# Three transformer blocks in one fp32 kernel on one Trainium2 core: the second block's down sections in the paired, token-major form

## The reference

```python
# second block
x = x + einsum('btc,cd->btd', merged, w_out)
h2 = rms_norm(x, norm2_g)
ff = square(relu(einsum('btd,df->btf', h2, w_ff1)))     # 2048 -> 8192
x = x + einsum('btf,fd->btd', ff, w_ff2)                # 8192 -> 2048
return rms_norm(x, final_g)
# third block: begins with rmsnorm(x, norm_mix_g), ends with
h = rmsnorm(x, norm_mlp_g)
x = x + square(relu(h @ w_up)) @ w_down
return rmsnorm(x, norm_final_g)
```

## Time and profile before

| what | value |
|---|---|
| median of three runs | 3273.06 us (3272.34 to 3274.05) |
| the profiled execution | 3272.41 us |
| its span | 3270.6 us, granted clock 0.999 |
| PE busy | 3248.7 us (99%), 21227 matmuls |
| PEld busy | 2816.8 us (86%) |
| DVE busy | 2264.7 us (69%), 3011 instructions |
| ACT busy | 1553.9 us (48%) |
| POOL busy | 359.0 us (11%) |
| DMA queue of the weights | 591.51 MB, 57.2% of 16 engines' span |

### The profile page before, as it was taken

The page is one execution under the profiler, slowest core; times in us unless marked ns, Lnnn a source line. Parts: engine busy times, 40 slices in busy tenths (PEclk is TensorE's granted clock), DMA queues, the critical chain, the costliest instruction groups (busy, mean ns, idle before and its releaser), DMA issues.

```text
span 3270.6 us, 51798 instructions
## 1 busy us (share of the span) xinstructions
PE 3248.7 (99%) x21227; PEld 2816.8 (86%) x21227; DVE 2264.7 (69%) x3011; ACT 1553.9 (48%) x2109; POOL 359.0 (11%) x356
## 2 busy tenths in 40 slices
PE   9999999999999999999999999999999999999999
PEld 8888888888878888888888888888888888888887
DVE  6468666567487667776665456656778777877787
ACT  5355434444554455445444444444455544544455
POOL 3000233310102003311000000012000100000000
PEclk9999999999999999999999999999999999999999
DMA  8455443446546557566656555665555555565555
GB/s 253 149 183 181 140 137 126 139 163 230 183 145 206 168 174 227 173 181 189 195 188 196 190 182 185 190 192 189 177 177 168 180 181 183 201 209 182 188 203 180
DMA packets 541729, 595.08 MB, mean 182 GB/s; under 512 B 25429, under 2 KB 484021, under 8 KB 540982
## 3 DMA queue, kind: packets, MB, share of 16 engines
q1 hardware_dynamic: 541350, 591.51, 57.2%
q10 hardware_dynamic: 144, 0.26, 0.0%
HBM read 585.32 MB, written 6.32 MB: 181 GB/s over the span
## 4 chain that ended last, share of the span: by engine, by line
PE 95%; DVE 3%; ACT 1%; issue 1%; POOL 0%; DMA 0%; SPq 0%; POOLq 0%; DVEq 0%; ACTq 0%
PE gp L3107 49%; PE gp L3111 26%; PE gp L2984 7%; PE gp L2990 4%; PE sidep L1340 3%; PE sidep L3009 1%; PE gp L3009 1%; PE sidep L3014 1%; DVE w_parts L2909 1%; PE gp L3014 1%; PE sidep L1626 0%; PE sidep L1630 0%; PE sidep L1908 0%; DMA high<-x 0%; PE sidep L2046 0%
## 5 line engine op out<-in xcount | busy, mean ns | idle before, releaser
L2909 DVE TENSOR_TENSOR w_parts<-ring,w_parts 128x1024 fp32r<-128x1024 f32 x1036 | 1305.3, 1285 | 250.3 <-ACT w_parts L2897 248.2
L3107 PE MATMUL gp<-x_parts,w_parts 128*128 128x512 f32 x5264 | 1296.6, 394 | 0.0
L2897 ACT ACTIVATE w_parts<-ring 128x1024 fp32r<-128x1024 f32 x1036 | 1058.0, 1052 | 302.3 <-PE gp L3107 125.1
L3107 PEld LDWEIGHTS gp<-x_parts,w_parts 128*128 128x128 f32 x5264 | 959.0, 188 | 186.0 <-issue 2.5
L3111 PEld LDWEIGHTS gp<-x_parts,w_parts 128*128 128x128 f32 x5264 | 684.7, 191 | 36.8 <-issue 4.9
L3111 PE MATMUL gp<-x_parts,w_parts 128*128 128x256 f32 x5264 | 708.4, 284 | 1.0 <-DVE w_parts L2909 0.4
L2317 ACT ACTIVATE lo_half<-gp 128x512 f32<-128x512 f32 x220 | 131.5, 598 | 721.2 <-PE gp L3107 586.5
L3107 PE MATMUL gp<-ff_parts,w_parts 128*128 128x512 f32 x1792 | 430.4, 391 | 0.0
L3107 PEld LDWEIGHTS gp<-ff_parts,w_parts 128*128 128x128 f32 x1792 | 328.9, 188 | 63.3
L2480 DVE TENSOR_TENSOR stage<-gp,lo_half 128x512 f32<-128x512 f32 x168 | 115.9, 690 | 291.4 <-ACT lo_half L2317 289.4
L3111 PEld LDWEIGHTS gp<-ff_parts,w_parts 128*128 128x128 f32 x1792 | 231.0, 191 | 10.4 <-issue 0.9
(11 more groups left out here) (435 smaller groups left out, 2640.7 us busy)
## 6 DMA issues: line engine op xcount, KB each, us to landing
ring<-w_in SPq DMA_DIRECT2D x440, 512.0 KB, 4.3
ring<-w_ff SPq DMA_DIRECT2D x256, 512.0 KB, 4.5
ring<-w_up SPq DMA_DIRECT2D x128, 512.0 KB, 4.2
ring<-w_down SPq DMA_DIRECT2D x128, 512.0 KB, 5.5
ring<-w_out SPq DMA_DIRECT2D x96, 512.0 KB, 4.4
ring<-w_branch_attn SPq DMA_DIRECT2D x16, 512.0 KB, 4.5
ring<-w_branch_rwkv SPq DMA_DIRECT2D x16, 512.0 KB, 4.8
gate_scratch<-stage SPq DMA_DIRECT2D x16, 256.0 KB, 2.2
```

What stands on the lines that cost most here:

```text
L2897: act.activation(w_parts[:, q % PARTS, 0], ring[:, u % RING, SLOT * half:SLOT * half + SLOT, :], ACT.Copy).then_inc(high_split, 1)
L2909: v.tensor_tensor(w_parts[:, q % PARTS, 1], ring[:, u % RING, SLOT * half:SLOT * half + SLOT, :], w_parts[:, q % PARTS, 0].bitcast(F32), A ...
L3107: return pe.matmul(gp[:, k % 2, j, :, :], w_parts[:, q % PARTS, 0, c, j * P:(j + 1) * P], operand(s, b, SLOT * n + c), start=(n == 0 and c ...
```

## The change

The down sections of the second block become `Paired`: token-major, two passes of 1024 features, six of the 16 pairs with seven products. Their row sums stand in two tiles of 128x512 (`turned_rows`: one for each 128 tokens), and since the second block's residual is kept feature-major, each of the four blocks of 512 features of a section is turned: when the block ends, VectorE adds the banks to the tiles (L2471, L2472 of the changed kernel), one slot later TensorE turns them with 8 fp32 transposes of 128x128 (`turned_tensor`, L2651), and VectorE adds the turned banks to `xt` in two instructions (`turned_vector`, L2659). The merges of the four shared products are other steps (`merge_products`). Behind `down2_1`, the norm's work follows each turned block: `turned_high` on ScalarE one and two slots after the end, `turned_low` on VectorE two and three after, the GpSimd adds one and two after; the places of the norm's thread and of `final2` are two slots later.

The `up2` sections make combined hidden blocks as the `up3` ones do. ScalarE's part of a combined block moves from phase 2 to phase 3 of the block's end in all four up sections. `MIXED` has another order, used by all paired sections, in which the first seven-product pair starts at slot 4 of a pass, not 2; `combine_weights` begins four slots ahead of the use, not three. In the inverse, level 5 uses 32x32 stationary tiles taken from `ab` directly, twice 64 products in all, and the GpSimd step `al5` (8 instructions) is gone. Storage for the combined blocks and the squares of the norm moves to other tiles; `last_rows` is now `x_rows` and larger. Each feature-major down section had 1024 matmuls, each paired one has 732 and 32 transposes.

```diff
@@ -307,7 +309,7 @@
         SEVEN = (1, 3, 6, 8, 10, 12)
-        MIXED, PLAIN = (0, 1, 2, 3, 4, 6, 5, 8, 7, 10, 9, 12), (11, 13, 14, 15)
+        MIXED, PLAIN = (0, 2, 1, 4, 3, 5, 6, 7, 8, 9, 10, 12), (11, 13, 14, 15)
         S, order = {}, []
@@ -337,7 +339,7 @@
             section(f"up2_{n}", 16, 16, columns(I["w_ff1_2"][0], 4096 * n))
-            section(f"down2_{n}", 8, 32, columns(I["w_ff2_2"][0], 0, 4096 * n))
+            add_section(Paired(f"down2_{n}", I["w_ff2_2"][0], 4096 * n, f"up2_{n}", MIXED, SEVEN, PLAIN))
         section("v3_0", 1, 16, wide_columns(w3, 0, 3072), wide=True)
@@ -1134,6 +1138,8 @@
+                        if l == 5:
+                            continue
@@ -1439,10 +1449,15 @@
-                        rw.po.wait(pe, f"al{l}", i)
+                        if l < 5:
+                            rw.po.wait(pe, f"al{l}", i)
...
+                                if l == 5:
+                                    m = mm(rw.x[quarter(o, 1), c * 32:(c + 1) * 32], rw.ab[quarter(s, 0), c, 32:64],
+                                           rw.xx[quarter(s, 0), 1, c, 0:32])
+                                    continue
@@ -1453,6 +1468,10 @@
+                                if l == 5:
+                                    m = mm(rw.x[quarter(o, 0), 256 + c * 32:256 + (c + 1) * 32], rw.yb[quarter(o, 1), c, 0:32],
+                                           rw.xx[quarter(o, 1), 0, c, 32:64])
+                                    continue
@@ -2331,11 +2361,11 @@
-            if phase == 2 and combined_after(s, b):
+            if phase == 3 and combined_after(s, b):
...
-                x, parts = combined_of(b)
+                x, parts = combined_of(s, b)
@@ -2436,7 +2464,13 @@
-                if phase == 0:
+                if phase == 0 and s.name.startswith("down2"):
+                    first, second = turned_rows(s)
+                    v.wait_ge(slot_used, block_end(s.name, b))
+                    v.wait_ge(rows_added, row_base(s, b // 2) + (3, 8)[b % 2])
+                    v.tensor_tensor(first, wide_sums(k, 0), first, ALU.add).then_inc(rows_added, 1)
+                    v.tensor_tensor(second, wide_sums(k, 1), second, ALU.add).then_inc(block_evacuated, 1)
+                elif phase == 0:
@@ -2556,18 +2590,35 @@
-            k, at_row = s.block0 + 2 * p, ROW_STEPS * pass_number(s, p)
+            k, at_row = s.block0 + 2 * p, row_base(s, p)
...
-            first, second = (combined_weights(s)[0][:, i] for i in range(2))
...
+            if step < 0:
+                return
...
-                if pass_number(s, p) == 0:
-                    v.wait_ge(out_copied, 8)
...
+            if s.name.startswith("down2"):
+                first, second = turned_rows(s)
+                if step == 0:
+                    v.tensor_copy(first, m1).then_inc(rows_added, 1)
+                    add(1, second, m6, first)
+                elif step == 1:
+                    add(2, second, m7, second)
+                elif step == 6:
+                    v.tensor_copy(first, m5).then_inc(rows_added, 1)
+                    add(5, first, m6, first)
+                elif step == 7:
+                    add(6, first, m1, first)
+                    add(7, second, m7, first)
+                return
+            first, second = (combined_weights(s)[0][:, i] for i in range(2))
+            if step == 0:
+                if at_row == row_base(S["down3_0"], 0):
+                    v.wait_ge(out_copied, 8)
@@ -2577,9 +2628,49 @@
-            else:
+            elif step == 3:
...
+        def turned_banks(s, b):
+            k = s.block0 + b
+            return (wide_sums(k, 0), wide_sums(k, 1)) if b % 2 == 0 else (sp_[:, 2, :], sp_[:, 3, :])
+        def turned_count(s, b):
+            return 4 * ("down2_0", "down2_1").index(s.name) + b + 1
+        def turned_tensor(pe, s, b):
+            pe.wait_ge(rows_added, row_base(s, b // 2) + (4, 9)[b % 2])
+            pe.wait_ge(block_evacuated, s.block0 + b + 1)
+            for j, bank in enumerate(turned_banks(s, b)):
+                for i in range(2):
+                    for t, part in enumerate(turned_rows(s)):
+                        m = pe.transpose(bank[:, i * TOK + t * P:i * TOK + t * P + P], part[:, (2 * j + i) * P:(2 * j + i + 1) * P], ident[:, :])
+            m.then_inc(out_turned, 1)
+        def turned_vector(v, s, b):
+            v.wait_ge(out_turned, turned_count(s, b))
+            for j, bank in enumerate(turned_banks(s, b)):
+                c = slice(4 * b + 2 * j, 4 * b + 2 * j + 2)
+                v.tensor_tensor(xt[:, c, :], bank.rearrange("p (c t) -> p c t", c=2), xt[:, c, :], ALU.add).then_inc(finished, 1)
+        def turned_high(act, s, n):
+            norm, gain, _ = next_norm[s.name]
+            act.wait_ge(finished, fin_count(s.name, n))
+            for c in (2 * n, 2 * n + 1):
+                m = act.activation(x_parts[:, c, 0, :], xt[:, c, :], ACT.Copy, scale=gains(gain, c))
+            m.then_inc(x_high_split, 1)
+            norm.square(act, n, xt[:, 2 * n:2 * n + 2, :], lambda i: par("final2", 2 * n + i))
+        def turned_low(v, s, n):
+            _, gain, xs0 = next_norm[s.name]
+            split_low_gained(v, n, gain, xs0 + n + 1)
@@ -2764,7 +2858,7 @@
-        threads.append(Thread("final2", at("v3_0") + 5.67, 1.0, vector=final2_vector))
+        threads.append(Thread("final2", at("v3_0") + 7.67, 1.0, vector=final2_vector))
@@ -2832,13 +2926,13 @@
-                if n > s.first_seven + 1:
+                if n > s.first_seven + 1 or b:
...
-                elif b == 0:
+                else:
...
-                else:
-                    v.wait_ge(rows_added, ROW_STEPS * pass_number(s, b) - 2)
+                if n == s.first_seven + 1 and b and s.name.startswith("down3"):
+                    v.wait_ge(rows_added, row_base(s, b) - 2)
@@ -3019,16 +3117,23 @@
-            k, number = s.block0 + 2 * b, pass_number(s, b)
+            k, number = s.block0 + 2 * b, PASSES.index((s.name, b))
...
+                if h == 0 and b and s.name.startswith("down2"):
+                    pe.wait_ge(finished, fin_count(s.name, 1))
...
-                if number:
-                    pe.wait_ge(rows_added, ROW_STEPS * (number - 1) + 7)
+                if number == 0:
+                    pe.wait_ge(n_copied, next_norm["out2"][0].copied)
+                elif number < 4:
+                    before, p = PASSES[number - 1]
+                    pe.wait_ge(finished, fin_count(before, 4 * p + 3))
+                elif number == 4:
+                    pe.wait_ge(out_copied, 8)
...
-                    pe.wait_ge(out_copied, 8)
+                    pe.wait_ge(rows_added, row_base(s, b) - ROW_STEPS + 7)
@@ -3052,6 +3157,9 @@
+                    for late in (1, 2):
+                        if turned_block(q, late) and turned_block(q, late)[0].name in next_norm:
+                            next_norm[turned_block(q, late)[0].name][0].add(pool, 2 * turned_block(q, late)[1] + late - 1)
@@ -3065,6 +3173,8 @@
+                    if turned_block(q, 1):
+                        turned_tensor(pe, *turned_block(q, 1))
@@ -3158,6 +3268,9 @@
+                    for late in (1, 2):
+                        if turned_block(q, late) and turned_block(q, late)[0].name in next_norm:
+                            turned_high(act, turned_block(q, late)[0], 2 * turned_block(q, late)[1] + late - 1)
@@ -3175,7 +3288,7 @@
                     side.run(q)
-                    combine_weights(v, q + 3)
+                    combine_weights(v, q + 4)
                     split_low(v, q + 2)
@@ -3183,6 +3296,11 @@
+                    if turned_block(q, 1):
+                        turned_vector(v, *turned_block(q, 1))
+                    for late in (2, 3):
+                        if turned_block(q, late) and turned_block(q, late)[0].name in next_norm:
+                            turned_low(v, turned_block(q, late)[0], 2 * turned_block(q, late)[1] + late - 2)
```

100 lines of the change are left out of this document (59 added, 41 removed).

## The result

The changed kernel takes 3254.92 us (median of 4 runs, 3254.65 to 3255.5) against 3273.06: a ratio of 0.9945, 95% interval 0.9933 to 0.9958. The forecast was 3252.5, 2.4 too low. The profiled execution took 3254.65 us, its span is 3252.9, so the span fell by 17.7.

The account below looks back on a forecast made before the run. The prediction took TensorE's issued work plus its waits for split weights as the bound (95% of the chain of waits). Its terms summed to -20.5 us, giving 3251.9 on the profiled execution and 3252.5 as median, range 3245 to 3261.

Parts of the forecast that it names:

- products of down2_0 and down2_1: Both down sections of the second block: 732 matmuls each at 0.2267 us, 331.8 against 357.5, so -25.7 us.
- eight turn groups: Output blocks of down2_0 and down2_1: eight transposes each, about 0.9 us per group on TensorE's path, +7.2 us.
- waits around the norm: down2_1 and v3_0: TensorE waits at second turns, the first seven-product pair and the norm's sums, +9 us, bounds 2 and 16.
- ScalarE's turn in up3: up3_0 and up3_1: weight split done before ScalarE's part of the combined hidden block, -1.7 us each, -3.4 together.
- down3: down3_0 and down3_1: combining a slot earlier and first seven-product pair two slots later remove waits, -4.6 us, bounds 0 and -5.1.
- level 5: Inverse: 128 products with 32-column instead of 64-column weights take less time per step, -3 us, bounds 0 and -4.2.
- the chain: down2_1 and v3_0: successive ScalarE, VectorE and GpSimd instruction times after a block's end, giving TensorE's waits, together +9 us.
- GpSimd's adds hold VectorE whole: Rival at down2_1's pass ends: VectorE stands until each GpSimd add ends, +10 us, 3262; chance 0.12.
- if the cover is missing: Case for the up sections: up2_0 and up2_1 cost +1.7 us each and the -3.4 of up3 is gone.
- The slower rival: Adjacent seven-product pairs in down2 and down3 leave VectorE 3.5 us behind per pass: +28, 3280.6 us; chance 0.05.
- my line: Inverse, level 5: step times at 128 and 64 columns extended to about 0.041 us at 32 columns, -37%.
- Boundaries covered: Rival at pass ends: ScalarE and VectorE have slots in hand, the +9 shrinks to 2 or 3, 3245 to 3246; chance 0.18.

Follow-up runs that it names:

- the small adds: Changed kernel with GpSimd's adds of squares for down2_1's norm over 8 columns instead of 512, most of the norm's sum left out: 3246.76 us.
- one slot more: Changed kernel with the norm work of down2_1 one slot later on ScalarE, GpSimd and VectorE, nothing left out: 3246.77 us, ratio 0.9920 to the kernel before.
- the kernel with two buffers: Changed kernel with two buffers in turn for the squares of down2_1's norm, GpSimd's adds whole: 3253.41 us.
- the all-plain one: Changed kernel with all 16 pairs plain in down2_0 and down2_1 (768 matmuls each instead of 732), turns kept: 3265.23 us.
- the spread one: Changed kernel with down2_1's norm work a slot later, two buffers for squares, and pass 1's second block's norm work at slots 14 and 20 of pass 2: 3244.27 us.
- the one with the slot and two buffers: Changed kernel with the norm work of down2_1 one slot later and two buffers for its squares: 3246.73 us.

## Why the prediction was right, and where not

By its own terms, from the lengths of the sections (predicted, measured):

| term | predicted | measured |
|---|---|---|
| products of down2_0 and down2_1 | -25.7 | -25.7 |
| eight turn groups | +7.2 | +7.2 |
| waits around the norm | +9 | +11.4 |
| ScalarE's turn in up3 | -3.4 | -2.9 |
| down3 | -4.6 | -5.1 |
| level 5 | -3 | -2.6 |
| sum, on the span | -20.5 | -17.7 |

**The products** came out because the paired form already ran in this trace, and its cadence of 0.2267 could be read. The turns cost 0.91 each in down2_0 and 0.86 in up2_1.

**The norm** is the term that was mis-sized, and most of the miss. Its waits in the changed kernel: 7.2 in down2_1 (175.9 less down2_0's 168.7) and 4.2 in v3_0 (5.03 less a turn). Link by link the chain had 2.1, 2.8, 2.4 and 1.9 (second turn of pass 1, last turn, first seven-product pair, sums); the waits listed are 2.9, 3.0, 3.3 and 1.2. The step that failed is the sentence that GpSimd's adds stretch a VectorE instruction by "about 0.5 an add". I had divided 6.3 us over twelve adds. As a mean that is not far off in the changed kernel either: its 16 low parts take 6.4 us more than with the small adds and its splits some 2, over 14 adds, 0.6 each. But the mean is no price for one place without a lead: the pair of adds ahead of the second turn cost VectorE 1.85 at once (2.72 against 0.87). A row of the kernel before says the same: beside a pair of adds, two splits took 3.70 there, where two alone take 2.35,

```profile
2141.60 3.70 DVE L2909 TENSOR_TENSOR w_parts<-ring,w_parts 128x1024 fp32r<-128x1024 f32 x2 [1.39 <-ACT w_parts L2897]
```

and GpSimd's pair took 3.52 there against 2.74 in the row shown above, where VectorE was the one held. Each waits for the other's instruction to end. That is the rival "GpSimd's adds hold VectorE whole", which I gave 0.12 and argued against with a mean. Its mechanism is the one at work (879 ns against 479 for the low parts); its price of +10 was too high, since I added it to a chain that was itself too long: without the adds 2.3 us of waits stay, where the chain has 6.6 without GpSimd's share (0.7 in the second pass and the 1.9 for the sums). Two errors of opposite sign made the term look good; that it came within 2.4 is luck. The Trainium skill, "SBUF — State Buffer", section "SBUF: two separate sides", states the lock, and that it takes in a VectorE instruction with two inputs in SBUF against a GpSimd instruction that reads SBUF. The trace agrees, also in the exception: a copy and an add that read PSUM took 0.68 and 0.69 as elsewhere, in the middle of GpSimd's pair of 2249.70 to 2253.22,

```profile
2252.00 0.68 DVE L2612 COPY x_rows<-sidep 128x512 f32<-128x512 f32 x1
2252.71 0.69 DVE L2598 TENSOR_TENSOR x_rows<-sidep,x_rows 128x512 f32<-128x512 f32 x1
```

The chain was also a link short: ScalarE's 1.88 for the buffer of squares stands in the order of the program and could have been read there.

**ScalarE's turn in the up sections** was right in mechanism and within 0.5 us (up3_1 lost the 1.7, up3_0 only 1.2); undoing it costs up2 the 1.7 each that "if the cover is missing" named (2.2 and 1.7).

**down3** was right in size, by a reason half right. The later first pair removes its wait; the fourth slot of lead is there for pairs 10 and 12. The slower rival's debt is real, its threshold was the right question, and the lead of 4.1 was enough. Its price assumed no lead at all.

**Level 5**: the rows give -2.7. By the rule of the Trainium skill ("TensorE: Matmul & The Clock Gate", section "LDWEIGHTS (loading the stationary operand)") that a weight load goes with the columns alone, the term would have been -4.2. A stretch of 32 matmuls by itself fell from 1.05 to 0.62 (-41%), between my line's -37% and the halving. The three stretches of 64 fell only from 2.08 to 1.44, since each now has a wait for ScalarE in its middle (0.23, 0.23 and 0.34), which the kernel before doesn't have and the prediction put at nothing:

```profile
670.57 0.33 PEld L1346 LDWEIGHTS sidep<-high 32*32 32x32 f32 x16 [0.23 <-ACT high L1302]
```

**Boundaries covered** (0.18, 3245 to 3246) did not happen in this kernel, yet it is about what one slot more reaches (3246.8).

## What to carry to other kernels

Before pairing a section with work on other engines, ask not for the mean stretch beside GpSimd but for single instructions: a lock of one whole instruction on an engine with no lead is paid in full, and with a lead cost almost nothing here. Where an in-order engine must wait for a result, put its next urgent work ahead of the wait, and place the rest at slots where the engines have a lead; here two moves of that kind and a second buffer gave 10.65 us beyond the change, 8.2 of it by the first move; the buffer brought nothing on top of it. And look at both halves of an edit that pays in one section only: here pairing down2_1 brought nothing until its norm was moved.

## What was not expected of the hardware

TensorE's granted clock fell from 1.00 to 0.50 (2.4 to 1.2 GHz) behind waits of 2.7 to 3.1 us in four of these kernels' profiles, for some 3 to 7 us. It didn't fall behind waits of 2.9 to 3.1 in three others, the changed kernel's among them, nor behind one of 3.4 in the kernel with two buffers. A fall took 1.7 to 3 us of TensorE's work, but what it cost hangs on what comes next: nothing in down2_1 and 0.8 in v3_0 of the kernel with the old level 5 (176.0 and 30.6 against 175.9 and 29.8), where a wait for other engines behind it shrank; about 2 in v3_0 of the all-plain one, where none was left to shrink (29.5 against the 24.5 of the spread one, of which 2.9 are waits). So a wait near 3 us may cost up to twice its length, and whether it does is open before the run. The totals don't tell: eight executions of the all-plain kernel lie between 3264.64 and 3266.49, and five of the one with the slot and two buffers, whose longest wait in the stretch is 2.2, between 3246.18 and 3247.88.
